# Decoder step on one core: RMS norms by exponential of half the negative logarithm instead of square root and reciprocal

## The reference

```
def rms_norm(x, g):
    y = x * lax.rsqrt(jnp.mean(x * x, axis=-1, keepdims=True) + EPS)     # EPS = 1e-6
    return y * g

for l in range(DEPTH):                                                   # DEPTH = 2
    x = x + rms_norm(token_mixer(rms_norm(x, g_pre_mix[l]), ...), g_post_mix[l])
    mk, mv = (rms_norm(mem, g_mem[l]) @ w for w in (w_xk[l], w_xv[l]))
    x = x + rms_norm(cross_attention(rms_norm(x, g_pre_x[l]), mk, mv, ...), g_post_x[l])
    x = x + rms_norm(conv_ffn(rms_norm(x, g_pre_ffn[l]), ...), g_post_ffn[l])

# in token_mixer: sliding-window attention with sinks, and 4 heads of a gated recurrence:
    logf = logaddexp(log(lb), log1p(-lb) + log_sigmoid(z));  k = (1 - lb) * sigmoid(-z);  q = silu(qr)
    o = o * lax.rsqrt(jnp.mean(o * o, axis=-1, keepdims=True) + EPS) * gn_l     # one norm per head
    o = o * silu(gr)
```

## Time and profile before

| | us |
|---|---|
| median of three executions | 3469.14 |
| lowest, highest | 3467.00, 3477.67 |
| the profiled execution | 3462.95 |
| its span, first to last instruction | 3461.2 |
| busy in the span: PE, weight loads, VectorE, ScalarE, GpSimd | 3247.4, 3077.2, 2324.1, 1185.9, 679.0 |
| 64 table loads on ScalarE | 1.283 each |

### The profile page before, as it was taken

How to read it: one execution, slowest core, us unless ns; L and a number is a source line. 1 busy time by engine, 2 the same in 40 slices (tenths; PEclk the granted TensorE clock), 3 DMA queues, 4 the chain that set the end, 5 groups by cost and what they waited for, 6 DMA issues and landing times. The chain is left out here.

```text
span 3461.2 us, 51914 instructions
## 1 busy us (share of the span) xinstructions
PE 3247.4 (94%) x21872; PEld 3077.2 (89%) x21872; DVE 2324.1 (67%) x3509; ACT 1185.9 (34%) x1849; POOL 679.0 (20%) x274
## 2 busy tenths in 40 slices
PE   7999889899899999999989998898998999999997
PEld 7998769788799999999889987698887999999996
DVE  6776782834467677777787767737345767777776
ACT  5342363434432222212344424533344222222212
POOL 1111131012312212222111111310123221212220
PEclk9999999999899999999999999999999999999998
DMA  5112223213411111111121122332044111111111
GB/s 177 44 44 63 76 80 128 75 43 119 183 50 43 49 43 55 39 54 43 54 82 40 50 68 73 107 111 73 26 158 157 43 50 43 49 43 55 40 57 52
DMA packets 71176, 245.87 MB, mean 71 GB/s; under 512 B 7969, under 2 KB 22561, under 8 KB 65825
## 3 DMA queue, kind: packets, MB, share of 16 engines
q1 hardware_dynamic: 70656, 242.50, 20.7%
q10 hardware_dynamic: 288, 0.06, 0.0%
HBM read 214.20 MB, written 23.04 MB: 69 GB/s over the span
## 5 line engine op out<-in xcount | busy, mean ns | idle before, releaser
L258 PE MATMUL ps<-hh,w_hi 128*128 128x344 f32 (+2 forms) x4320 | 1417.6, 328 | 84.1 <-DVE w_lo L252 26.0
L260 PE MATMUL ps<-hh,w_lo 128*128 128x344 f32 (+2 forms) x4320 | 1391.2, 322 | 0.0
L259 PE MATMUL ps<-hl,w_hi 128*128 128x344 f32 (+2 forms) x4320 | 1391.0, 322 | 0.0
L243 POOL TENSOR_TENSOR w_lo<-w_raw,w_hi 128x1024 fp32r<-128x1024 f32 x270 | 678.8, 2516 | 2719.6 <-ACT w_hi L235 2719.6
L258 PEld LDWEIGHTS ps<-hh,w_hi 128*128 128x128 f32 x4320 | 822.8, 190 | 112.8 <-issue 53.5
L259 PEld LDWEIGHTS ps<-hl,w_hi 128*128 128x128 f32 x4320 | 822.0, 190 | 3.2 <-issue 1.1
L260 PEld LDWEIGHTS ps<-hh,w_lo 128*128 128x128 f32 x4320 | 822.0, 190 | 0.0
L2591 DVE TENSOR_TENSOR Y<-Y,ps 128x344 f32<-128x344 f32 x912 | 433.2, 513 | 155.7 <-PE ps L260 155.7
L235 ACT ACTIVATE w_hi<-w_raw 128x1024 fp32r<-128x1024 f32 x296 | 310.6, 1052 | 440.6 <-PE ps L260 383.8
L2390 ACT ACTIVATE f_c<-f_u,cT 128x1032 f32<-128x1032 f32 (+1 forms) x92 | 111.4, 1213 | 634.6 <-DVE f_u L2556 628.0
L259 PE MATMUL ps<-f_glo,w_hi 128*128 128x344 f32 x960 | 308.0, 321 | 0.0
(11 more groups left out here) (356 smaller groups left out, 3730.0 us busy)
## 6 DMA issues: line engine op xcount, KB each, us to landing
w_raw<-in_w_stream SPq DMA_DIRECT2D x296, 512.0 KB, 3.5
out_y_cols<-xT SPq DMA_DIRECT2D x9, 1376.0 KB, 6.3
xT<-out_y_cols SPq DMA_DIRECT2D x2, 4128.0 KB, 14.0
mem_keys<-in_cache_mem_k SPq DMA_DIRECT2D x8, 1024.0 KB, 5.0
mem_values<-in_cache_mem_k SPq DMA_DIRECT2D x8, 1024.0 KB, 6.3
mem_keys<-in_cache_mem_v SPq DMA_DIRECT2D x8, 1024.0 KB, 5.1
mem_values<-in_cache_mem_v SPq DMA_DIRECT2D x8, 1024.0 KB, 6.9
xT<-in_x_cols SPq DMA_DIRECT2D x3, 1376.0 KB, 12.4
```

The source lines that it names most:

```text
L243: nc.gpsimd.tensor_tensor(w_lo[:, SLOT[m], :], w_raw[:, m % RR, :], w_hi[:, SLOT[m], :].bitcast(F32), ALU.subtract).then_inc(lo_done["pool ...
L258: nc.tensor.matmul(out, whi, mhi, start=start, stop=False)
L259: nc.tensor.matmul(out, whi, mlo, start=False, stop=False)
L260: return nc.tensor.matmul(out, wlo, mhi, start=False, stop=stop)
```

## The change

ScalarE takes the inverse root by two activations, Ln(sum/D + eps) and then Exp(-0.5 * that), so no square root and no wide reciprocal is left; the small reciprocals of the softmaxes stay. Both functions are in one table set, which is loaded by name at fixed places of ScalarE's program: once at the start, behind the first Silus of a mixer, behind the Ln of each later head's gates and behind its Silus, and in place of the dummy Sqrt at the end of the MLP. The Ln of the gates is still served by a set that the compiler picks. For "pre" norms the Exp writes rs directly, so the roots behind them no longer wait for their slot of the two-buffer tile; for the heads the semaphore of the roots counts two instead of one, one for the prompt's and one for the samples' root. On VectorE the reciprocals go and the waits for the roots stay.

```diff
+        def load_log_exp():
+            nc.scalar.preload_act_table_set("natural_log_exp_and_others")
+
+        def inverse_root(out, log, total, n, ready):
+            act_c(nc.scalar.activation(log, total, ACT.Ln, bias=epst[:], scale=1.0 / n))
+            nc.scalar.activation(out, log, ACT.Exp, scale=-0.5).then_inc(ready, 1)
...
@@ mixer, first norm (layer 0) @@
-                        nc.scalar.activation(roots[c], ps[:, BA + c, 0:CH], ACT.Sqrt, bias=epst[:], scale=1.0 / D)\
-                            .then_inc(s["root0"], 1)
+                        inverse_root(rs[:, cols(c)], roots[c], ps[:, BA + c, 0:CH], D, s["root0"])
...
-                        nc.vector.reciprocal(rs[:, cols(c)], roots[c]).then_inc(s["rs"], 1)
-                        dve.wait_ge(s["rs"], c + 1)
...
@@ mixer, ScalarE @@
                         split_hi(act, load0 + 6)
+                        load_log_exp()
                         exp_level(0, 1)
...
                             gates(r + 1)
+                            load_log_exp()
                             split_hi(act, load0 + base + 5)
...
                             silus(r + 1)
+                            load_log_exp()
                             split_hi(act, load0 + base + 6)
...
-                        act_c(nc.scalar.activation(bl[:], ps[:, BB, 0:NB], ACT.Sqrt, bias=epst[:], scale=1.0 / P))
-                        nc.scalar.activation(sq8[:], ps[:, BC, 272:272 + NS], ACT.Sqrt, bias=epst[:],
-                                             scale=1.0 / P).then_inc(s["root"], 1)
+                        inverse_root(bl[:], bl[:], ps[:, BB, 0:NB], P, s["root"])
+                        inverse_root(sq8[:], sq8[:], ps[:, BC, 272:272 + NS], P, s["root"])
...
@@ mixer, VectorE @@
-                        dve.wait_ge(s["root"], r + 1)
-                        dve_c(nc.vector.reciprocal(bl[:], bl[:]))
+                        dve.wait_ge(s["root"], 2 * r + 1)
...
-                        dve_c(nc.vector.reciprocal(sq8[:], sq8[:]))
+                        dve.wait_ge(s["root"], 2 * r + 2)
...
@@ output and query stage; the cross stage in the same way @@
+                            kind, c = MEANS[i]
                             act.wait_ge(mean_ready, i + 1)
-                            if i >= 2:
-                                act.wait_ge(rt_used, i - 1)
-                            n = C3[MEANS[i][1]][1]
-                            nc.scalar.activation(rt[:, i % 2, 0:n], ps[:, 3, 0:n], ACT.Sqrt, bias=epst[:], scale=1.0 / D)\
-                                .then_inc(rt_ready, 1)
+                            if i >= 2 and MEANS[i - 2][0] == "post":
+                                act.wait_ge(rt_used, sum(k == "post" for k, _ in MEANS[:i - 1]))
+                            r = rt[:, i % 2, 0:C3[c][1]]
+                            inverse_root(r if kind == "post" else rs[:, cols(c)], r, ps[:, 3, 0:C3[c][1]], D, rt_ready)
...
-                            dve_c(nc.vector.reciprocal(r, r))
...
@@ End @@
-                        nc.scalar.activation(rs[:, cols3(c)], ps[:, 6 + e % 2, 0:CH], ACT.Sqrt, bias=epst[:], scale=1.0 / D)\
-                            .then_inc(self.s["root"], 1)
+                        inverse_root(rs[:, cols3(c)], rs[:, cols3(c)], ps[:, 6 + e % 2, 0:CH], D, self.s["root"])
...
-                        dve_c(nc.vector.reciprocal(rs[:, cols3(c)], rs[:, cols3(c)]))
...
-                    nc.scalar.activation(warm[:], epst[:], ACT.Sqrt)
+                    load_log_exp()
```

More of the change, by code:

```diff
@@ L298, in root @@
                     act.wait_ge(s["mean"], 1)
-                    nc.scalar.activation(mrs[:], ps[:, 7, 0:NMEM], ACT.Sqrt, bias=epst[:], scale=1.0 / D).then_inc(s["root"], 1)
+                    inverse_root(mrs[:], mrs[:], ps[:, 7, 0:NMEM], D, s["root"])
                 def scale(self, dve):
                     dve.wait_ge(s["root"], 1)
-                    dve_c(nc.vector.reciprocal(mrs[:], mrs[:]))
             def sync(sp):
@@ L675, in stage_mixer @@
                 s = {n: sem(f"hg_{n}") for n in (
-                    "spilled", "hh", "hl", "sq", "sum", "mean0", "root0", "rs", "part", "out",
+                    "spilled", "hh", "hl", "sq", "sum", "mean0", "root0", "part", "out",
                     "sp", "k", "lnf", "silu", "e", "exp", "x", "lvl", "lvl_used", "vt", "vt_copied", "vdiag", "eb", "xs", "kh", "kt",
@@ L1599, in root @@
                             dve.wait_ge(rt_ready, i + 1)
-                            r = rt[:, i % 2, 0:C3[MEANS[i][1]][1]]
-                            dve_c(nc.vector.reciprocal(r, r))
                         def normalise(i):
@@ L1609, in normalise @@
                                 .then_inc(rt_used, 1)
-                            dve.wait_ge(rt_used, i + 1)
+                            dve.wait_ge(rt_used, c + 1)
                         def residual(c, ks):
@@ L1631, in scale @@
                         def scale(i):
-                            c = MEANS[i][1]
                             dve.wait_ge(rt_ready, i + 1)
-                            nc.vector.reciprocal(rs[:, cols(c)], rt[:, i % 2, 0:C3[c][1]]).then_inc(rt_used, 1)
-                            dve.wait_ge(rt_used, i + 1)
                         def low_slab(i):
@@ L1838, in stage_cross_ffn @@
                 UP_CHUNKS = sorted(range(NCH), key=LAST_IN_BANK.get)
-                warm = ph.enter_context(nc.sbuf_tensor(f"f_warm{l}", [P, 1], F32))
                 def cols3(c):
@@ L1851, in stage_cross_ffn @@
                     EVENTS += [("pre", 0), ("post", 2), ("pre", 1), ("pre", 2)] if l + 1 < DEPTH else [("post", 2)]
-                    s = {n: sem(f"e_{n}") for n in ("sq", "sum", "root", "x", "hh", "hl", "rs", "norm", "whole", "tree", "mean")}
+                    s = {n: sem(f"e_{n}") for n in ("sq", "sum", "root", "x", "hh", "hl", "norm", "whole", "tree", "mean")}
                     added = 24 * (FT - 2)
@@ L2000, in scale @@
                     def scale(self, dve, e):
-                        c = self.EVENTS[e][1]
                         dve.wait_ge(self.s["root"], e + 1)
-                        nc.vector.reciprocal(rs[:, cols3(c)], rs[:, cols3(c)]).then_inc(self.s["rs"], 1)
-                        dve.wait_ge(self.s["rs"], c + 1)
                     def vector(self, dve, low):
@@ L2318, in root @@
                     def root(i):
+                        kind, c = MEANS[i]
                         act.wait_ge(s["mean"], i + 1)
-                        if i >= 2:
-                            act.wait_ge(s["rt_used"], i - 1)
-                        w = C3[MEANS[i][1]][1]
-                        nc.scalar.activation(rt[:, i % 2, 0:w], ps[:, mean_bank(i), 0:w], ACT.Sqrt, bias=epst[:], scale=1.0 / D)\
-                            .then_inc(s["root"], 1)
+                        if i >= 2 and MEANS[i - 2][0] == "post":
+                            act.wait_ge(s["rt_used"], sum(k == "post" for k, _ in MEANS[:i - 1]))
+                        r = rt[:, i % 2, 0:C3[c][1]]
+                        inverse_root(r if kind == "post" else rs[:, cols(c)], r, ps[:, mean_bank(i), 0:C3[c][1]], D, s["root"])
                     def high(c, ks):
@@ L2471, in normalise @@
                             .then_inc(s["rt_used"], 1)
-                        dve.wait_ge(s["rt_used"], i + 1)
+                        dve.wait_ge(s["rt_used"], c + 1)
                     def residual(c):
@@ L2488, in scale_of @@
                     def scale_of(i):
-                        c = MEANS[i][1]
                         dve.wait_ge(s["root"], i + 1)
-                        nc.vector.reciprocal(rs[:, cols(c)], rt[:, i % 2, 0:C3[c][1]]).then_inc(s["rt_used"], 1)
-                        dve.wait_ge(s["rt_used"], i + 1)
                     top(0)
```

## The result

The changed kernel takes 3443.08 us, the median of 4 runs (3441.15 to 3447.89), against 3470.01 for the kernel before on the same chip (4 runs, 3467.0 to 3477.67): 0.9921 of its time, with a 95% interval of 0.9902 to 0.994. That is 26.9 us by the medians. Its profiled execution took 3441.15 us (span 3439.3), 21.8 less than that of before. In a second comparison it took 3441.91 (5 runs) against 3466.04: 0.9929, interval 0.9917 to 0.9942.

What follows compares the result with a forecast made beforehand. PE, busy 94% of the span, was taken as the bound, so time could be won only where it stands still, some 214 us. Terms summing to 24.2 us, taken from the median 3469.14, gave 3445.0 us; range 3435 to 3457.

Steps and rivals of the forecast that it cites:

- start: Kernel start: a table load and first reciprocal go, PE's gaps of 2.00 and 0.94 close; gain 2.9 us.
- heads, both layers: Heads: only head 3's spread comes sooner for PE, 0.2 us per layer; gain 0.4 us in total.
- window stages: Window stages: without the table load before the first softmax VectorE starts earlier; 1.05 us per layer, 2.1 in all.
- output and query: Output and query stage: of 6.9 us of reciprocals ahead of late slabs 3.8 arrive per layer; gain 7.6 us.
- cross stages: Cross stages: PE waits for the last root, now also for its Exp; loss 0.48 us per layer, 0.96.
- hand-over: Hand-over of layers: six reciprocals go, the first hidden, the other five walked through; gain 6.5 us, bounds 4.3 and 8.8.
- last stage: Last stage: first reciprocal hidden by PE, second gives 1.85 us and third 2.30; gain 4.15 us.
- clock: Whole kernel: shorter gaps should give back some of PE's granted clock in five places; gain 1.5 us, bounds -2 and 6.
- rival 3: Table switches: the skill's drain is real but not in the rows; 2.8 us more gain, 3442.2 us, chance 0.02.
- rival 1: Two middle stages: VectorE's freed time is covered by other waits; only 9.2 us gained, 3460 us, chance 0.12.
- Rival 2: Every root: named load does not hold, two loads placed at each; 15 us slower, 3484 us, chance 0.04.
- Rival 4: Norm stages: PE's clock recovers fully, VectorE's savings arrive nearly whole; 34 us less, 3435 us, chance 0.06.

Runs made afterwards that it cites:

- that with halves: Changed kernel with the slab's low part moved ahead and ScalarE's eight high parts written in two halves around that slab's split: 3435.91 us, 0.9907 of before.
- the short low parts: Changed kernel with GpSimd's low parts in the second layer's hand-over and heads written in 8 of 1024 columns only: 3428.87 us, 0.988 of before.

## Why the prediction was right, point by point

Forecast 3445.0, measured 3443.08. The table gives it by parts, in us won, from PE's shifts: the first pair of traces is the profiled runs of before and after, the second pair the second traces. The heads end at 400 and 2110 us, the second window stage at 2250.

```text
                          predicted   first pair   second pair
start                        2.9          2.35         1.65
heads, both layers           0.4         -1.9         -0.75
window stages                2.1          4.8          2.7
output and query             7.6          7.2          8.5
cross stages                -1.0         -0.75        -2.8
hand-over                    6.5          5.85        10.4
last stage                   4.15         4.2          4.2
clock                        1.5     (in the rows above)
sum                         24.2         21.8         23.8
```

**Start.** The gap of 2.00 closed as worked out (2.1 and 1.8 us are won there); 0.9 of the first pair's 2.35 stands ahead of PE's first product, where the two traces of before differ by as much. The step that failed is "whose 0.94 also closes": the fourth reciprocal, 1.74 us, was gone, but VectorE's next operation took 2.36 instead of 0.29, since it now met a low part on GpSimd of 62.05 to 64.45.

```profile
62.12 2.36 DVE L1130 TENSOR_SCALAR hg_fs<-hg_set,oml,lbt 128x8 f32<-128x8 f32 x1
...
62.05 2.40 POOL L243 TENSOR_TENSOR w_lo<-w_raw,w_hi 128x1024 fp32r<-128x1024 f32 x1 [6.96 <-ACT w_hi L235]
```

Before, the reciprocal had run beside that low part (64.32 to 66.75) and took no longer for it, nor did the low part:

```profile
64.77 1.74 DVE L303 RECIPROCAL mrs<-mrs 128x256 f32<-128x256 f32 x1
...
64.32 2.43 POOL L243 TENSOR_TENSOR w_lo<-w_raw,w_hi 128x1024 fp32r<-128x1024 f32 x1 [7.05 <-ACT w_hi L235]
```

So an operation that doesn't collide was replaced by nothing, and one that collides moved into its place.

**Heads.** The gain of 0.2 at the last head isn't there: its gap is 1.79 before and after the earlier trace rows, because the spread ahead of it stands behind GpSimd in both kernels (3.17 and 3.40 us for an operation of 1.23), and beginning sooner it only stands longer. Both pairs show a small loss, of the size of one or two dips of the clock. In the first trace after, 1.7 us of it is the dip near 185 us, with PE busy and no gap; the second trace lacks it.

**Window.** The mechanism was right and the term too small: 1.05 per layer was taken, and the load put back costs 1.2 and 1.8 at its place. What the first pair has beyond that in its 4.8 is not the change's, as the second pair shows. Behind the load the next activation starts 0.02 us later, in the kernels with placed loads and in that without the name. The 1380 ns of drain that the Trainium skill (ScalarE: Activation LUTs, What ACT_TABLE_LOAD costs) adds to a switch are in no row here, and rival 3 falls as a mechanism, though its 3442.2 is nearer to the measured time (0.9 us off) than my own number (1.9 off).

**Output and query.** 3.8 per layer was walked out, 4.2 and 4.3 came in the first layer, and 4.1 and 3.9 in the kernel with this part alone. With the 3.4 us added back that PE had won before this stage, unit 4 begins at 649.3, walked out as 649.35, and unit 7 at 666.8, walked out as 667.15. In the second layer the first pair shows only 3.0: PE loses 0.9 ahead of the reciprocals (at 2339 us), where the second trace of before loses 1.1 against the first as well. The 5.50 stayed, as said. The walk also had 3.1 of 6.9 us lost to other waits: that is why the last gap is still 2.61.

**Cross.** The wait for the last root went from 0.66 to 1.12, by 0.46, for a predicted 0.48. What the second pair loses beyond that lies in the clock: its dips from 800 to 1000 and from 2500 to 2680 us cost 1.7 and 3.4 us more in the trace after, while PE's waits for the cache's transfers are the same or shorter (26.2 us before, 24.9 after).

**Hand-over.** 6.5 was predicted, 5.85 found in the first pair, 10.4 in the second. From 1690 to 1850 us the changed form takes 5.85 to 7.0 us less than the first trace of before in seven traces, and 4.4 in an eighth, that with halves; it is the old form that varies, since it collides with GpSimd in three of its four traces (2.0 us), and in the same three a dip of the clock falls on PE's dense units behind the third mean, where in the first trace of before the dip (1765.7 us) comes ahead of it, under a wait. The walk was made on the one trace that escaped both. So the term is 6 to 10, and the upper bound of 8.8 was too low. In the time this is hidden, because the sum was set against the median of before, 6.2 us above the profiled run.

**Last stage.** 4.15 was predicted, and 4.2 came in both pairs, in the predicted places and all of it behind PE's last product.

**Clock.** This step has nothing behind it. Adding up the stretches in which the records show 1.2 GHz, without the tail behind PE's last product, PE lost 58.0 us in both traces of before and 59.7 and 63.1 in those after. Nothing was given back; shorter gaps did not mean fewer dips.

**The rivals.** Of rival 1 (covered, 3460) the 5.50 gap and 3.1 us of the walk were true, not the rest. Rival 2 (slower, 3484) is what happens without the name: 3481. Rival 4 (3435) is not seen. The sum came out right although its parts were up to 3.9 us too small and up to 2.3 too large: the errors had both signs, and that they cancel this well is luck. What was not luck is the mechanism: with the reciprocals kept the gain is gone, and the start's gap, the output stage and the last stage gave what their steps worked out.

## What to carry to other kernels

Take an inverse root as Ln and Exp on ScalarE when VectorE is the late engine: a reciprocal of 2.3 us left its order here and an activation of 0.49 came to ScalarE's. But it pays only with one set loaded by name, without which the same code is slower than before. Before a term is read from one trace, lay a second one of the same kernel beside it: product by product they differ by up to 4.5 us in one stage. And where VectorE and GpSimd both work from SBUF, look for single operations far above their group's time; they tell who holds up whom, and what time freed on VectorE will run into.

## What the runs showed of the hardware

- **VectorE beside GpSimd.** An elementwise operation of VectorE from SBUF that begins while a 128x1024 one of 2.4 us runs on GpSimd is longer by about what that one still has to run: where it began 0.1 to 0.4 us behind it, 0.29 became 2.36, 0.52 became 2.54 and 1.23 became 3.40, and 1.0 us behind it 3.36 became 4.64. In the other order GpSimd's operation took 4.20 us instead of 2.40. In the two traces of before, the two of the changed kernel and that with the short low parts, every operation of VectorE that is over 0.7 us longer than the shortest of its kind (same names and shape, in any trace) overlaps one of GpSimd. In one layer's hand-over and heads this costs 13 us of 3442 by the medians, about 10 by PE's shift against the two traces of the changed kernel (10.0 and 11.2, while the clock's dips there differ by 1.0 against and 1.7 for the short low parts). What such operations are too long adds up to 222 and 224 us in the traces of before and to 241 and 245 in those after: this is where some 18 of the 87.7 us went that the reciprocals left free. Eleven wide reciprocals of before run in part beside GpSimd, and none of them is longer for it. The row of before that tells it, the four low parts that take 6.28 us where four others take 2.04, I had read as work:

```profile
1717.43 2.04 DVE L1089 SCALAR_TENSOR_TENSOR hl<-xT,gT,hh 128x344 fp32r<-128x344 f32 x4
...
1720.95 6.28 DVE L1089 SCALAR_TENSOR_TENSOR hl<-xT,gT,hh 128x344 fp32r<-128x344 f32 x4
```

- **The clock's dips.** The stretches at 1.2 GHz last 3.4 us and more in the traces, and one of 3.4 under a busy PE costs 1.7 us. There are 20 to 31 in an execution, some always in the same place (behind the gaps of the window stage), some in one execution and not in the next of the same kernel, as that at 185.31 us. Of the 4.0 us between the two traces of the changed kernel they are 3.4, and of the 5.9 between the two of before they are nothing by their sum, though one of them fell where PE had no wait to cover it.
- **A load of tables** costs 1.28 us placed or by name. The next activation starts 0.01 to 0.02 us behind it where it waits for nothing else, as at the 53 loads ahead of an Exp in the kernel without the name.
